# One more quad of the MLP down projection in the seven-product form, and new places for the sums it needs

## The reference

```python
def squared_relu_mlp(h, w_up, w_down):
    a = jnp.square(jax.nn.relu(h @ w_up))
    return a @ w_down

for layer in range(DEPTH):
    h = rmsnorm(x, ln_mix_g[layer])
    x = x + (sb_fox_mixer if layer % 2 == 0 else mla_mixer)(h, ...)
    h = rmsnorm(x, ln_mlp_g[layer])
    x = x + squared_relu_mlp(h, mlp_w_up[layer], mlp_w_down[layer])
```

## Time and profile before

| | us |
|---|---|
| median of 3 runs | 2067.74 (2067.7 to 2068.05) |
| the profiled execution | 2067.2 |
| its span | 2065.5 |
| TensorE (matmul) busy | 2053.9, 99% of the span |
| VectorE busy | 1456.6, 71% |
| ScalarE busy | 1099.1, 53% |
| GpSimd busy | 214.9, 10% |

### The profile page before, as it was taken

The page is one execution under the profiler, slowest core; times in us unless marked ns, Lnnn a source line. Parts: engine busy times, 40 slices in busy tenths (PEclk is TensorE's granted clock), DMA queues, the critical chain, the costliest instruction groups (busy, mean ns, idle before and its releaser), DMA issues.

```text
span 2065.5 us, 26109 instructions
## 1 busy us (share of the span) xinstructions
PE 2053.9 (99%) x10336; PEld 1741.9 (84%) x10336; DVE 1456.6 (71%) x1957; ACT 1099.1 (53%) x1578; POOL 214.9 (10%) x317
## 2 busy tenths in 40 slices
PE   8999999999999999999999999999999999999999
PEld 7888888888888888888888898888888888888887
DVE  5556555566876876786697788557786696687777
ACT  5555565454544544554566676444554464454454
POOL 0000000020210120010010155001110021012000
PEclk9999999999999999999999999999999999999999
DMA  8554554595786796597575543468696588679565
GB/s 272 179 164 163 163 165 162 184 264 185 237 283 196 225 277 208 186 283 234 192 231 189 157 128 123 163 199 250 198 306 209 184 264 265 199 226 291 182 196 191
DMA packets 219985, 432.32 MB, mean 209 GB/s; under 512 B 13964, under 2 KB 20184, under 8 KB 219864
## 3 DMA queue, kind: packets, MB, share of 16 engines
q1 hardware_dynamic: 198312, 380.29, 55.4%
q0 software_dynamic: 21504, 50.34, 10.7%
q10 hardware_dynamic: 48, 0.02, 0.0%
HBM read 428.52 MB, written 2.10 MB: 208 GB/s over the span
## 4 chain that ended last, share of the span: by engine, by line
PE 98%; DVE 1%; DMA 1%; ACT 1%; issue 0%; SPq 0%; DVEq 0%; ACTq 0%
PE psum L1609 23%; PE psum L1539 14%; PE psum L1541 14%; PE psum L1540 14%; PE psum L1612 11%; PE psum L1843 5%; PE psum L1841 5%; PE psum L1842 5%; PE psum L1682 1%; PE psum L1769 1%; DMA raw<-in_mlp_w_down 1%; PE psum L1627 1%; PE psum L1746 0%; PE psum L1582 0%; DVE halves L1068 0%; PE psum L1770 0%
## 5 line engine op out<-in xcount | busy, mean ns | idle before, releaser
L1068 DVE TENSOR_TENSOR halves<-raw,halves 128x1024 fp32r<-128x1024 f32 (+1 forms) x724 | 850.3, 1182 | 446.6 <-ACT halves L763 442.3
L763 ACT CAST halves<-raw 128x1024 fp32r<-128x1024 f32 (+1 forms) x724 | 724.7, 1014 | 609.1 <-PE psum L1541 287.6
L1609 PE MATMUL psum<-h,halves 128*128 128x512 f32 x2048 | 639.0, 395 | 0.0
L1612 PEld LDWEIGHTS psum<-h,halves 128*128 128x128 f32 x2048 | 380.1, 188 | 87.7
L1612 PE MATMUL psum<-h,halves 128*128 128x256 f32 x2048 | 397.9, 278 | 0.0
L1539 PE MATMUL psum<-halves,a 128*128 128x512 f32 x828 | 325.7, 393 | 0.4 <-DVE halves L1068 0.4
L1541 PE MATMUL psum<-halves,a 128*128 128x512 f32 x828 | 322.7, 390 | 0.0
L1540 PE MATMUL psum<-halves,a 128*128 128x512 f32 x828 | 322.3, 389 | 0.0
L1609 PEld LDWEIGHTS psum<-h,halves 128*128 128x128 f32 x2048 | 314.3, 189 | 2.8
L1539 PE MATMUL psum<-halves,h 128*128 128x512 f32 (+1 forms) x508 | 201.3, 396 | 0.4 <-DVE halves L1068 0.4
L1541 PE MATMUL psum<-halves,h 128*128 128x512 f32 (+1 forms) x508 | 194.9, 384 | 0.0
(11 more groups left out here) (266 smaller groups left out, 2090.1 us busy)
## 6 DMA issues: line engine op xcount, KB each, us to landing
raw<-in_mlp_w_up SPq DMA_DIRECT2D x128, 1024.0 KB, 5.8
raw<-in_mlp_w_down SPq DMA_DIRECT2D x128, 1024.0 KB, 5.3
mix<-in_mlp_w_down POOLq DMA_DIRECT2D x192, 256.0 KB, 7.1
raw<-in_sf_w_in SPq DMA_DIRECT2D x45, 1024.0 KB, 5.1
raw<-in_sf_w_o SPq DMA_DIRECT2D x16, 1024.0 KB, 5.1
raw<-in_mla_w_o SPq DMA_DIRECT2D x16, 1024.0 KB, 5.2
raw<-in_mla_w_down SPq DMA_DIRECT2D x8, 1024.0 KB, 5.4
raw<-in_mla_w_ukv SPq DMA_DIRECT2D x8, 1024.0 KB, 5.7
```

The costliest lines, as they stand in the source:

```text
L763: nc.scalar.copy(half_piece(n, 0), raw_piece(n)).then_inc(hi_done, 1)
L1068: v.tensor_tensor(half_piece(n, 1), raw_piece(n), half_piece(n, 0).bitcast(F32), ALU.subtract)\
L1609: last = mm(bank, half_piece(n, 0)[:, cols], src[:, k].rearrange("p s t -> p (s t)"), start=(k == 0), stop=(k == KT - 1))
L1612: last = mm(bank[:, T:2 * T], half_piece(n, 1)[:, cols], src[:, k, 0], start=False, stop=False)
```

## The change

q5 becomes a fast quad; q2 stays plain. So a block has 78 pieces in place of 76 and seven gathered sums in place of six. The fast quads are then q0, q1, q3, q4, q5, q6, q7. Their sums are gathered in the buffers 2, 0, 1, 3, 2, 0, 1, so that the last three use those of the first three again. The token sums of one more quad are made in the third chunk's shadow, in a buffer that was made twice as large (`sd_nat`). The queue of GpSimd loads for the next block now begins with a buffer that `combine` uses. The diff, cut to its core:

```diff
-FAST_QUADS = 0, 1, 3, 4, 6, 7
-PLAIN_QUADS = 2, 5
-U_BUFFER = 0, 1, 2, 3, 0, 1
+FAST_QUADS = 0, 1, 3, 4, 5, 6, 7
+PLAIN_QUADS = 2,
+U_BUFFER = 2, 0, 1, 3, 2, 0, 1
+ENDS_CHUNK = 0, 2, 3, 5
...
-        with nc.sbuf_tensor("sd_nat", [P, 4, 2, P], F32R) as sd_nat:
+        with nc.sbuf_tensor("sd_nat", [P, 2, 4, 2, P], F32R) as sd_nat:
...
-                elif m < 2:
+                elif m in (1, 2):
                     pool.wait_ge(lo_done, base - BLOCK_PIECES + quad_at(FAST_QUADS[m + 4]) + 2)
                 else:
                     pool.wait_ge(x_added, (ADDED_MLP0, ADDED_MLP1)[layer] + 4 * (b0 - 1) + 3)
...
-                    for m in (0, 2, 4):
+                    for m in (0, 2):
                         u_load(layer, b0, m)
                         u_load(layer, b0, m + 1)
                         u_add(layer, b0, m)
                         u_add(layer, b0, m + 1)
+                    u_load(layer, b0, 4)
+                    u_add(layer, b0, 4)
+                    u_load(layer, b0, 5)
+                    u_load(layer, b0, 6)
+                    u_add(layer, b0, 5)
+                    u_add(layer, b0, 6)
...
-                        if c == 1 and j == 2:
-                            token_sums(no, 1)
-                        if c == 1 and j == 4:
-                            token_sums_lo(no, 1)
+                        if c in (1, 3) and j == 2:
+                            token_sums(no, ENDS_CHUNK[c - 1] + 1)
+                        if c in (1, 3) and j == 4:
+                            token_sums_lo(no, ENDS_CHUNK[c - 1] + 1)
...
-                sums = {34: 0, 37: 1, quad_at(2) - 3: 2, quad_at(3) - 1: 3, quad_at(5) - 2: 4, quad_at(6) - 1: 5}
+                sums = {34: 0, 37: 1, quad_at(2) - 3: 2, quad_at(3) - 1: 3, quad_at(4) - 1: 4, quad_at(5): 5, quad_at(6) - 1: 6}
```

More of the change, by code:

```diff
@@ L131, in summed_count @@
 def summed_count(layer, b0, m):
-    return 32 * (3 * block_no(layer, b0) + m // 2 + 1)
+    return 32 * ((4, 3)[m % 2] * block_no(layer, b0) + m // 2 + 1)
 def stepped_count(layer, b0, m):
-    return 2 * (6 * block_no(layer, b0) + m + 1)
+    return 2 * (7 * block_no(layer, b0) + m + 1)
 def quad_at(q):
@@ L430, in sd_of @@
         def sd_of(i):
-            return sd[:, i] if i < 4 else (sd_last, sd_nat)[i - 4][:]
+            return sd[:, i] if i < 4 else sd_nat[:, i - 5] if i > 4 else sd_last[:]
         def out_on_pool(n):
@@ L1010, in token_sums_hi @@
             def token_sums_hi(no, i):
-                act.wait_ge(a_step, 24 * no + 4 * i + 4)
+                act.wait_ge(a_step, 28 * no + 4 * i + 4)
                 nc.scalar.copy(sd_of(i)[:, :, 0], a_sum).then_inc(sd_hi, 1)
@@ L1020, in mlp_block @@
                         split_hi(base + 8 * c + j + AHEAD)
-                        if c == 1 and j == 3:
-                            token_sums_hi(no, 1)
+                        if c in (1, 3) and j == 3:
+                            token_sums_hi(no, ENDS_CHUNK[c - 1] + 1)
                         if b0 == 0 and c == 0 and j == 2:
@@ L1028, in mlp_block @@
                     nc.scalar.copy(a[:, 4 * c:4 * c + 4, 0, :], y_buf).then_inc(y_hi, 1)
-                    token_sums_hi(no, c + 1 if c else 0)
+                    token_sums_hi(no, ENDS_CHUNK[c])
                 for j in range(32, BLOCK_PIECES):
@@ L1033, in mlp_block @@
                     if j == 34:
-                        token_sums_hi(no, 5)
+                        token_sums_hi(no, 6)
                     for at, slot, bank in ((quad_at(7) - 1, 3, X8), (quad_at(7), 0, X1)):
@@ L1037, in mlp_block @@
                             act.wait_ge(pieces_used, base + at + 1)
-                            act.wait_ge(lo_done, base + quad_at(FAST_QUADS[3]) + 2)
+                            act.wait_ge(lo_done, base + quad_at(FAST_QUADS[4]) + 2)
                             nc.scalar.copy(c_sum[:, slot], bank).then_inc(joint_copied, 1)
@@ L1389, in token_sums @@
             def token_sums(no, i):
-                done = 24 * no + 4 * i
+                done = 28 * no + 4 * i
                 if done:
@@ L1403, in token_sums_lo @@
             def token_sums_lo(no, i):
-                dve.wait_ge(sd_hi, 6 * no + i + 1)
+                dve.wait_ge(sd_hi, 7 * no + i + 1)
                 v.tensor_tensor(sd_of(i)[:, :, 1], a_sum, sd_of(i)[:, :, 0].bitcast(F32), ALU.subtract)                 .then_inc(sd_ready, 1)
@@ L1459, in mlp_block @@
                         if c and j == 1:
-                            token_sums_lo(no, c if c > 1 else 0)
-                        if c == 1 and j == 2:
-                            token_sums(no, 1)
-                        if c == 1 and j == 4:
-                            token_sums_lo(no, 1)
+                            token_sums_lo(no, ENDS_CHUNK[c - 1])
+                        if c in (1, 3) and j == 2:
+                            token_sums(no, ENDS_CHUNK[c - 1] + 1)
+                        if c in (1, 3) and j == 4:
+                            token_sums_lo(no, ENDS_CHUNK[c - 1] + 1)
                         if b0 == 0 and c == 0 and j == 2:
@@ L1478, in mlp_block @@
                                     ALU.subtract).then_inc(split_done, 1)
-                    token_sums(no, c + 1 if c else 0)
-                sums = {34: 0, 37: 1, quad_at(2) - 3: 2, quad_at(3) - 1: 3, quad_at(5) - 2: 4, quad_at(6) - 1: 5}
+                    token_sums(no, ENDS_CHUNK[c])
+                sums = {34: 0, 37: 1, quad_at(2) - 3: 2, quad_at(3) - 1: 3, quad_at(4) - 1: 4, quad_at(5): 5, quad_at(6) - 1: 6}
                 end = quad_at(8)
@@ L1500, in mlp_block @@
                     if j == 33:
-                        token_sums_lo(no, 4)
-                        token_sums(no, 5)
+                        token_sums_lo(no, 5)
+                        token_sums(no, 6)
                     if j == 35:
-                        token_sums_lo(no, 5)
+                        token_sums_lo(no, 6)
                     if j in sums:
@@ L1904, in mlp_block @@
                             if q in FAST_QUADS:
-                                pe.wait_ge(sd_ready, 6 * no + FAST_QUADS.index(q) + 1)
+                                pe.wait_ge(sd_ready, 7 * no + FAST_QUADS.index(q) + 1)
                                 fast_quad(base + quad_at(q), q, added0 + 1)
```

## The result

| | before | after |
|---|---|---|
| median of 5 runs each, on one chip | 2067.7 (2066.32 to 2068.05) | 2075.76 (2075.49 to 2076.45) |
| the profiled execution | 2067.2 | 2075.49 |
| its span | 2065.5 | 2073.7 |

The account below looks back on a forecast made before the run. TensorE's matmul count bounds the kernel while VectorE keeps up; in the quads VectorE falls behind. Waits cost 1.72 a block, matmuls return 0.68: +8.3 over eight, less 0.9, 2067.7 + 7.4 = 2075.1 us; range 2071.5 to 2079.

Parts of the forecast that it names:

- Matmuls: In the quads, q5 has 21 matmuls in place of 24: 0.68 us less a block, 5.44 over eight.
- Step 1: At q5's start in block 2, two additions delay its first split to 717.44; TensorE waits 0.26 us.
- Step 2: From q5's first split to q7's, VectorE takes 10.72 us plus 0.15; TensorE starts q7 at 729.58.
- Step 3: From q7's start, 4.76 us of matmuls and a 0.11 restart: quads end at 734.45, +1.04 us a block.
- handover from VectorE to TensorE: In the quads, TensorE starts 0.05 us behind the end of a VectorE split it waits for.
- Where the waits fall: In the quads, on the first pieces of q5, q6 and q7, largest at q7, about 1.4 us plus restarts.
- The 0.86 us at the blocks' ends: TensorE's waits ending two layer 0 blocks go as GpSimd's DMAs move later: 0.86 us gained, at worst none.
- Rival A: In the quads, VectorE keeps up and the waits do not come: 2061.4 us; chance 0.08.
- Rival B: In the quads, free restarts and handovers 0.1 to 0.2 shorter: waits about 1.1 us a block, 2070.2; chance 0.07.
- Rival C: q7's gathered sum lands late and stops VectorE: 4.1 us spare; one late gives 2083, worst 2105; chance 0.08.
- Rival D: VectorE's operations do not overlap, so its quad work takes 0.8 us more: +1.8 a block, 2081.6; chance 0.02.
- Rival E: The change doesn't do what it says, for instance the seven products wait for token sums; no size; chance 0.02.

Follow-up runs that it names:

- no_adds: The changed kernel with VectorE's two additions left out for q5, q6 and q7, every other instruction kept: 2061.2 us, ratio 0.9969.
- one_wait: The changed kernel with TensorE waiting once for all seven quads' token sums, ahead of the first quad, not ahead of each: 2075.95 us, one run.
- late_gather: The kernel before, with all loads for the next block's sums waiting for `x_added`: 2065.74 us, one run.
- spread: The changed kernel with VectorE's additions moved earlier: q3's by one piece, q4's and q5's by four, q6's by three: 2112.98 us, ratio 1.0219.
- earlier: The changed kernel with VectorE's additions moved earlier: q4's by one piece, q5's by four, q6's by one: 2069.19 us, ratio to the kernel before 1.0011.
- pool_adds: The changed kernel with the additions for q5, q6 and q7 made by GpSimd, behind its adding DMAs: 2105.82 us, ratio 1.0187.

## Why the prediction was right

Point by point, the times of the changed trace less the 1.18 us by which its quads start later (695.15 against 693.97):

- **Matmuls**, -5.44: exact. `no_adds` has quads of 38.76 and blocks of 171.50 us, 0.68 under block 6 of the earlier trace rows.
- **Step 1**: q5's first split starts at 717.42 (predicted 717.44). TensorE starts at 718.79, predicted 718.71.
- **Step 2**: q7's first split starts at 728.33 (predicted 728.31). The 10.72 + 0.15 between the two splits is 10.91. This is what the forecast rested on: VectorE's starts as rates, and the order of its row. TensorE starts q7 at 729.69, predicted 729.58.
- **Step 3**: the quads end at 734.56, predicted 734.45. From q7's start to there it is the predicted 4.87, with the restart's 0.11 made up of 0.08 in the next start and 0.03 in those that follow. So quads of 40.59 against 40.48, +1.15 a block against +1.04.
- **The term that was mis-sized** is the handover from VectorE to TensorE, 0.05 in steps 1 and 2. The prediction shows no row for that figure. It belongs to pieces with one wait in front (0.05 in the changed kernel too, at q6's second piece: 725.24 + 1.22 to 726.51). In front of a quad's first piece it is 0.15 (`one_wait`). On q7's start, which alone counts, that is 0.09 of the 0.11 a block, and so most of the difference between +9.2 and +8.3.
- **Where the waits fall** was told wrong for q6. Its additions stand behind its first split, not ahead of it, as the prediction's own order rows showed; so its wait is at its second piece. The sum didn't hang on it, as the prediction said.
- **The 0.86 us at the blocks' ends**: gained in full by the windows, and reproduced alone by `late_gather`.
- **The token sums in the fourth chunk**: 22.31 us, nothing.
- **Rival A** (VectorE keeps up, 2061.4) is what `no_adds` gave, 2061.2: its arithmetic held, its premise didn't, since VectorE has no idle row from q5 to q7. The distance between 2061.2 and 2075.8 is the price of 1.33 us of additions in three quads.
- **Rival B** (cheaper handovers and restarts): the handover costs more, not less. Its price was wrong too: the prediction's sum holds one handover of 0.05 and one restart of 0.11, so with both at nothing the waits are still 1.56 us a block, not 1.1, and the time is 2073.8, not 2070.2. The stretch of the range below 2073.6 had no ground in it.
- **Rival C** (q7's gathered sum late): 3.6 us to spare, predicted 4.1. But `spread` shows what it would have been: one addition that waits for a landing stops all of VectorE.
- **Rival D** (operations do not overlap) would have made step 2 0.8 us longer. The split of 718.60 runs 1.22 us and the next operation starts 1.14 behind it in the same trace; the measurement decides against it for this kind of row. The prediction left out half of what the Trainium skill says in "VectorE: DVE Perf Modes", section "The DRAIN you can't avoid": it goes on that a next operation that is not held starts earlier. These rows agree with that half.
- **Rival E** (the quads wait for their token sums): the last of a block's token sums is ready at 690.2, ahead of the quads (695.15), and `one_wait`, which waits for all seven ahead of q0, has shorter quads.

Why the change loses is then plain. A fast quad saves TensorE 0.68 us and costs VectorE 5.36 against 2.28, 3.08 more. That is free as long as VectorE's row has slack in reach of four buffers, and the plain q5 was this slack. Without it the shortfall of 0.60 a quad runs over q3 to q7, and whatever is short arrives as a wait. No order of additions tried here brings the seven-quad form under the six-quad one: the best, `earlier`, is at 1.0011. Rounding was on ScalarE, with 28 of 40 us busy; a split that costs VectorE less was not tried, nor was another choice of the plain quad.

## What to carry to other kernels

Before you shorten the engine that is busy 99%, add up per stage what the edit gives the engine that feeds it, by the distance between starts and not by durations, and compare it with the feeder's margin in buffers: here a 71% share hid a stage at 89%. Move work ahead on the feeder only as far as its inputs have landed by then; an instruction too early blocks its whole engine, which in `spread` cost 37 us against the changed kernel where 8 were to be saved (of the 37, some 9 came with the lower clock). And a second engine is no place for the work if it slows the first one down while it runs.

## What the runs showed of the hardware that was not expected

- Two semaphore waits ahead of a matmul, of which the second is late, cost it 0.09 to 0.10 us more than one: 0.15 and 0.05 from the end of VectorE's split to TensorE's start (`after` and `one_wait`, q5's and q7's first pieces).
- A restart of TensorE after a short wait costs 0.08 to 0.11 us in the next start (0.31 to 0.34 in place of 0.227): 0.31 where two waits stood in front of the first matmul, 0.34 where one did.
- GpSimd's additions stretch VectorE's two-input operations beside them by 1.1 to 2.2 us each, and take 1.71 and 1.91 us in the mean themselves for 128x512 beside VectorE's work, against 0.69 on VectorE alone.
- After a wait of some 3 us TensorE can come back at the lower of its two clocks (1.2 GHz, not 2.4). In `spread`, with 2.69 us idle ahead of it, in the third block:

```profile
909.73 0.80 PE L1850 MATMUL psum<-halves,sd_last 128*128 128x512 f32 x1 [2.69 <-DVE halves L1075]
910.33 0.63 PE L1851 MATMUL psum<-halves,sd_last 128*128 128x512 f32 x1
910.75 0.63 PE L1852 MATMUL psum<-halves,sd_last 128*128 128x512 f32 x1
```

```profile
909.70:912.50 2.80, 2.77 (x7) 2.19 (x8) 2.80 (x3) 0.00 (x0) 0.00 (x0) 0.50 0.93 216
```

The starts are 0.427 apart and the granted clock is 0.50. In block 2 of the same kernel a wait of 3.46 us (start to start) was followed by full speed, so a wait of this length does not always bring it. In `pool_adds` it came in four of the eight blocks, each with one distance of 2.94 to 3.01 us, at once in two of them and a few matmuls behind it in the other two. The changed kernel's waits, 0.3 to 0.8 us, never did: its clock is 1.00 in all windows.
